# Down projections of a two-layer decoder step: 512 tokens in one matmul, the 8 sample tokens by a second, narrow path

## The chip, the cores and the metric

The kernel runs on one core of one Trainium2 chip. The metric is the device time of one execution in microseconds (us), here the median of several runs. Five engines matter: TensorE (PE in the profile, with its weight loads as a row of their own, PEld), VectorE (DVE), ScalarE (ACT), GpSimd (POOL) and SyncE (SP), which issues nearly all of the DMAs.

## The reference, cut to what matters

A group of 512 prompt tokens and a group of 8 sample tokens go through two layers with shared weights. Each layer has two feed-forward blocks, one ahead of the token mixer and one behind it:

```
D_MODEL, D_FF, SEQ = 1024, 2816, 512          # 8 sample tokens beside the 512
def swiglu(h, wg, wu, wd):
    return (jax.nn.silu(h @ wg) * (h @ wu)) @ wd

xp = xp + 0.5 * swiglu(rmsnorm(xp, norm_ffn1[i]), ffn1_wg[i], ffn1_wu[i], ffn1_wd[i])
xs = xs + 0.5 * swiglu(rmsnorm(xs, norm_ffn1[i]), ffn1_wg[i], ffn1_wu[i], ffn1_wd[i])
# then the mixer (attention in layer 0, a convolution module in layer 1),
# then the same once more with ffn2, then a gated per-layer input embedding
```

The product with `wd` (2816 x 1024) is the down projection. There are four of them: `down1` and `down2` of both layers. All inputs are fp32.

## The kernel before

**Layout.** The 520 tokens lie along the free dimension, features along the 128 partitions. `x` is `[128, 8, 520]`, the hidden values of a feed-forward block are `[128, 22, 520]` (22 groups of 128 features, `KF`).

**Arithmetic.** A product of fp32 values is made of three products of a format, fp32r, that TensorE takes in one pass: each operand is split into a high and a low part, and hi x hi, hi x lo and lo x hi are summed in PSUM (`products`, L253). The weights are split in the kernel: ScalarE copies a slab of raw weights into `w_hi` (`split_hi`, L238), and VectorE subtracts to get `w_lo` (`split_lo`, L242). A plain fp32 matmul, which the kernel uses in smaller places, is issued by the compiler as two instructions, so that for instance the 2 matmuls of `stat_pe` (L289) are 4 rows of the trace; a transpose stays one.

**Token halves.** A PSUM bank holds 512 fp32 columns, and 520 tokens don't fit. So each output tile takes two banks, 260 tokens in each, and each of the three products of a k group is issued twice, once for each half, with the same weights: 6 matmuls of 260 columns for each group of 128 features, each with its own weight load.

**A down projection** makes 8 output tiles (m) of 128 features. The weights of a tile come in two slabs of 11 k groups (`KH`; 128 x 1408 values). A slab is thus 66 matmuls, a projection 16 slabs and 1056 matmuls, and the four projections 64 slabs and 4224 matmuls. Two buffers `w_raw`, `w_hi` and `w_lo` (j = 0, 1) take the slabs in turn, and two PSUM slots (s = 0, 1; two banks each) take the tiles in turn.

**Who waits for whom in a down projection.** There is no planner; the order is written out for each engine, with counting semaphores between them.

- SP (`to_x_sp`, `load_slab`, L232): the load of slab n waits for `slab_lo`, until slab n - 2, which has the same buffer, is split. All weight loads of the kernel go through this one queue in order.
- ACT (`to_x_act`): `split_hi` of slab n waits for its landing and for `slab_used`, until PE is through with slab n - 2. Once a tile there are also `h_hi` (L264) and a square (L266) of the finished x tile.
- DVE (`to_x_dve`): in each tile two `split_lo`, `add_to_x` (L310), which adds half of the PSUM tile to x, and `h_lo` (L270) for the next stage.
- PE (`down_pe`): waits for `evac` of the tile that last had the slot, then for `slab_lo` and `a_lo_ok` of each slab, and issues `products`.

The last tile of a projection is evacuated during the first slab of the stage behind it (`after_to_x`), and the hidden values of the last group of an up stage (`after_up`) during the first slab of the down projection.

**Plain fp32 with quarters of the columns.** The kernel has places where a weight operand of 32 columns is used and the output goes to 32 of the 128 PSUM partitions, with the quarter g changing from one matmul to the next: `sample_values` (L962) in the attention and `taps_pe` (L1573) in the convolution. Both move 512 columns.

Of the kernel before, what the change touches and what calls it, by code (L numbers as in the profile page):

```python
# [5 lines left out]
F32 = mybir.dt.float32  # L6
# [42 lines left out]
def build(nc, io):  # L49
# [4 lines left out]
    with ctx:  # L54
# [35 lines left out]
        minus_bias = sb("minus_bias", [P, NH])  # L90
        eps = sb("eps", [P, 2])
        pages = sb("pages", [1, NS * PG], I32)


        def phase_memory(*specs):
# [6 lines left out]
            ("taps_j", [P, 4, KD, GROUPS], F32))  # L102
        a_hi, a_lo = phase_memory(("a_hi", [P, KF, T], F32R), ("a_lo", [P, KF, T], F32R))
        (o_hi, o_lo, k_f, sg_p, sg_m, a_t, kc, vc, zs, runs, aw) = phase_memory(
# [35 lines left out]
        def slot(s):  # L140
            return ps[:, s, :, 0:HALF]

        def flat(s, b=0):
# [40 lines left out]
        tap4_in = sem("tap4_in")  # L184
        ident4_ok = sem("ident4_ok")


        at = {}
        slab = tile = norm = hid = xt = fn = 0
        for layer in range(2):  # L190
            for name in (("load",) if layer == 0 else ()) + ("up1", "down1", "mix", "mixout", "up2", "down2", "ple"):
                at[name, layer] = dict(slab=slab, tile=tile, norm=norm, hid=hid, xt=xt, fn=fn)
                if name == "load":
# [8 lines left out]
                if name[:4] == "down":  # L202
                    slab += 2 * KD
                    tile += KD
                    xt += KD
                if name == "mix":
                    n = 3 * NP if layer == 0 else 2 * KD
                    slab += n
                    tile += n
                    fn += 0 if layer == 0 else KD  # L210
                    norm += 1
# [15 lines left out]

        def load_slab(sp, n, j, src, kt):

            sp.wait_ge(slab_lo, n - 1)  # L230
            dst = w_raw[:, j, 0:kt * P].rearrange("p (k c) -> p k c", k=kt)
            sp.dma_start(dst, src).then_inc(slab_in[j], 16)  # L232
# [12 lines left out]
        def products(pe, out, j, w0, kts, hi, lo, k0, first, last, wait_k=None, token_halves=(0, 1)):  # L245
# [168 lines left out]
        def to_x_sp(sp, a, spt, w, loaded=0):  # L414
            n0 = a["slab"]
            with sp.Fori(loaded // 2, KD * spt // 2) as step:
                m = 2 // spt * step
                for j in range(2):
                    src = slab_src(w, m, j * KH, KH) if spt == 2 else slab_src(w, m + j)
                    load_slab(sp, n0 + spt * m + j, j, src, KH if spt == 2 else KD)  # L420

# [26 lines left out]
        def to_x_dve(dve, a, spt, layer, which, factor, prev_evac, prev_lo):  # L448
# [5 lines left out]
            if spt == 2:  # L454
                def step(m, s):

                    split_lo(dve, n0 + 2 * m, 0, cols)
                    add_to_x(dve, s, n0 + 2 * m - 1, m - 1, factor)
                    split_lo(dve, n0 + 2 * m + 1, 1, cols)
                    x_post_dve(dve, a, layer, which, m - 1)  # L460
# [21 lines left out]
        def down_pe(pe, a, hidden):  # L482
            n0, t0 = a["slab"], a["tile"]
            with pe.Fori(0, KD // 2) as half:
                m = 2 * half
                for s in range(2):
                    pe.wait_ge(evac, t0 + m + s - 1)
                    for c in range(2):
                        pe.wait_ge(slab_lo, n0 + 2 * (m + s) + c + 1)
                        pe.wait_ge(a_lo_ok, hidden + KH * (c + 1))  # L490
                        products(pe, slot(s), c, 0, range(KH), a_hi, a_lo, c * KH, c == 0, c == 1).then_inc(slab_used, 1)

# [85 lines left out]

        def load_dve(dve):
            def x_in(m):  # L580
                dve.wait_ge(load_t, m + 1)
# [31 lines left out]
        def after_to_x(a, spt, layer, which, factor):  # L613
# [8 lines left out]
            def dve_evac(dve):  # L622
                def run_(j):
                    m = KD - 2 + j
                    if spt == 1 or j == 1:
                        add_to_x(dve, m % 2, a["slab"] + spt * (m + 1) - 1, m, factor)
                return run_
# [112 lines left out]
        def attn_sp(sp):  # L740
# [20 lines left out]
            for m in range(NP):  # L761
                load_slab(sp, n0 + m, m % 2, qkv_src(0, m), KD)
            sp.wait_ge(first_in[3], 16)
# [742 lines left out]
        def conv_sp(sp):  # L1506
            n0 = C["slab"]

            def both(k):
                for c in range(2):  # L1510
                    src = io["conv_w_in"][0].rearrange("(k p) f -> p k f", p=P)[:, :, ds(c * D + k * P, P)]
                    load_slab(sp, n0 + 2 * k + c, c, src, KD)

# [419 lines left out]
        def ple_sp(sp, a, layer):  # L1933
            n0 = a["slab"]
            for g in range(2):
                src = io["ple_w_proj"][layer].rearrange("(k p) f -> p k f", p=P)[:, :, g * 4 * P:(g + 1) * 4 * P]
                sp.wait_ge(slab_lo, n0 + g - 1)
                sp.dma_start(w_raw[:, g, 0:KP * 4 * P].rearrange("p (k c) -> p k c", k=KP), src).then_inc(slab_in[g], 16)
            with sp.Fori(0, KD // 2) as half:
# [290 lines left out]
```

## Time and profile before

| | |
|---|---|
| median of 3 runs | 2304.34 us (2300.72 to 2305.11) |
| the profiled execution, its own time | 2306.85 us |
| its span in the trace | 2305.1 us |
| PE busy | 2207.5 us, 96% of the span |
| DVE / ACT / POOL busy | 1099.3 / 752.8 / 152.4 us |
| mean granted TensorE clock | 0.981 of full speed |
| read from and written to HBM | 229.25 and 9.86 MB |

The trace is of one execution. Starts are recorded; ends of matmuls are modelled and neighbours overlap, so the pace of PE is read from the distance between starts, not from durations. In the timeline view neighbouring instructions of one line and one pair of operands are merged: the first column is the start of the first one, the second the time to the end of the last one, and "x2" their count. The clock column of the window view is the granted TensorE clock: 1.00 is 2.4 GHz, 0.50 is 1.2 GHz.

### The profile page before, as it was taken

The numbers are of one execution on the slowest core, as the hardware profiler recorded it, in microseconds if no ns is written. First come the engines' busy times: TensorE is split into PE (matmuls) and PEld (weight loads), VectorE is DVE, ScalarE is ACT, GpSimd is POOL, SyncE is SP. The second block draws the span as 40 slices with busy tenths as digits, with TensorE's granted clock in tenths as the row PEclk, the third lists the DMA queues.
The fourth block names the chain that finished last, engine by engine and source line by source line (L and its number), as shares of the span: only waits on it lengthen the run. The fifth ranks groups of instructions, "written<-read, shape, count | busy, mean of one in ns | idle before, by whom it ended". The sixth has DMA issues, their size and how long they took to land.

```text
span 2305.1 us, 43436 instructions
## 1 busy us (share of the span) xinstructions
PE 2207.5 (96%) x17957; PEld 2105.6 (91%) x17957; DVE 1099.3 (48%) x1280; ACT 752.8 (33%) x1012; POOL 152.4 (7%) x117
## 2 busy tenths in 40 slices
PE   7999999978998999999999999999798899999998
PEld 7999999967777999999999999999565899999998
DVE  5444433378884444443355444433635644443344
ACT  4222222446663422222234222222111532222223
POOL 2000001010000100000110000001302100000100
PEclk9999999989998999999999999999899899999999
DMA  3333332425663333333232333333454233333322
GB/s 115 91 91 91 105 88 81 156 92 186 218 229 112 100 91 91 91 105 88 81 92 83 91 91 91 100 92 90 125 124 118 58 92 91 91 91 101 93 71 83
DMA packets 379914, 240.30 MB, mean 104 GB/s; under 512 B 8506, under 2 KB 362394, under 8 KB 379832
## 3 DMA queue, kind: packets, MB, share of 16 engines
q1 hardware_dynamic: 371128, 234.89, 34.5%
q10 hardware_dynamic: 8704, 4.26, 0.6%
q8 instruction: 59, 0.97, 0.2%
q14 instruction: 23, 0.19, 0.0%
HBM read 229.25 MB, written 9.86 MB: 104 GB/s over the span
## 4 chain that ended last, share of the span: by engine, by line
PE 83%; DVE 7%; issue 4%; DMA 3%; ACT 2%; POOL 1%; ACTq 0%; SPq 0%; DVEq 0%; POOLq 0%
PE ps L253 79%; DVE sg_m L1341 1%; DMA g_rows<-g_pad 1%; DVE kc L1357 1%; PE ps L1573 1%; DVE w_lo L242 1%; PE ps L1969 1%; DVE sg_p L1348 1%; DVE zs L1362 1%; DMA g<-g_rows 1%; POOL log_ms L1918 0%; PE ps L825 0%; DMA w_raw<-in_attn_w_qkv 0%; ACT w_hi L238 0%; DVE h_lo L270 0%
## 5 line engine op out<-in xcount | busy, mean ns | idle before, releaser
L253 PE MATMUL ps<-h_hi,w_hi 128*128 128x260 f32 x3712 | 757.6, 285 | 15.0 <-DVE w_lo L242 10.4
L253 PE MATMUL ps<-h_hi,w_lo 128*128 128x260 f32 x3712 | 749.9, 284 | 0.0
L253 PE MATMUL ps<-h_lo,w_hi 128*128 128x260 f32 x3712 | 748.6, 283 | 0.0
L238 ACT ACTIVATE w_hi<-w_raw 128x1024 fp32r<-128x1024 f32 (+1 forms) x314 | 353.9, 1127 | 1122.5 <-PE ps L253 1092.2
L253 PEld LDWEIGHTS ps<-h_hi,w_hi 128*128 128x128 f32 x3712 | 575.3, 189 | 27.7 <-DVE w_lo L242 12.2
L253 PEld LDWEIGHTS ps<-h_hi,w_lo 128*128 128x128 f32 x3712 | 574.0, 189 | 0.0
L253 PEld LDWEIGHTS ps<-h_lo,w_hi 128*128 128x128 f32 x3712 | 573.0, 189 | 0.0
L242 DVE TENSOR_TENSOR w_lo<-w_raw,w_hi 128x1024 fp32r<-128x1024 f32 (+1 forms) x316 | 420.3, 1330 | 270.9 <-ACT w_hi L238 270.4
L253 PE MATMUL ps<-a_hi,w_hi 128*128 128x260 f32 x1408 | 283.9, 283 | 0.0
L253 PE MATMUL ps<-a_hi,w_lo 128*128 128x260 f32 x1408 | 283.2, 282 | 0.0
L253 PE MATMUL ps<-a_lo,w_hi 128*128 128x260 f32 x1408 | 282.7, 282 | 0.0
L304 DVE TENSOR_TENSOR s_up<-ps,rms 128x520 f32<-128x520 f32 x108 | 75.5, 699 | 321.5 <-PE ps L253 315.3
L253 PEld LDWEIGHTS ps<-a_lo,w_hi 128*128 128x128 f32 x1408 | 217.2, 188 | 0.0
L253 PEld LDWEIGHTS ps<-a_hi,w_hi 128*128 128x128 f32 x1408 | 216.8, 188 | 0.0
L253 PEld LDWEIGHTS ps<-a_hi,w_lo 128*128 128x128 f32 x1408 | 216.6, 188 | 0.0
L304 DVE TENSOR_TENSOR s_gate<-ps,rms 128x520 f32<-128x520 f32 x116 | 81.1, 699 | 187.4 <-PE ps L253 148.0
L310 DVE SCALAR_TENSOR_TENSOR x<-ps,x 128x520 f32 (+1 forms) x42 | 29.4, 700 | 199.9 <-PE ps L253 199.9
L283 POOL TENSOR_TENSOR sumsq<-sumsq,square 128x520 f32<-128x520 f32 x56 | 87.4, 1560 | 480.4 <-ACT square L266 450.1
L328 ACT ACTIVATE a_hi<-s_prod 128x520 f32 (+1 forms) x88 | 56.2, 639 | 176.2 <-DVE s_prod L335 176.2
L337 DVE TENSOR_TENSOR a_lo<-s_prod,a_hi 128x520 f32 (+1 forms) x88 | 61.6, 700 | 80.7 <-ACT a_hi L328 80.7
L280 POOL COPY sumsq<-square 128x520 f32<-128x520 f32 x8 | 6.8, 852 | 1384.7 <-ACT square L266 1360.0
L270 DVE SCALAR_TENSOR_TENSOR h_lo<-x,gains,h_hi 128x520 fp32r<-128x520 f32 (+1 forms) x64 | 80.5, 1266 | 3.4 <-ACT h_hi L264 2.0
(224 smaller groups left out, 1588.5 us busy)
## 6 DMA issues: line engine op xcount, KB each, us to landing
w_raw<-in_ffn_wg SPq DMA_DIRECT2D x88, 512.0 KB, 3.8
w_raw<-in_ffn_wu SPq DMA_DIRECT2D x88, 512.0 KB, 3.8
w_raw<-in_ffn_wd SPq DMA_DIRECT2D x64, 704.0 KB, 4.4
kc<-in_cache_k SPq DMA_DIRECT2D x32, 512.0 KB, 5.5
vc<-in_cache_v SPq DMA_DIRECT2D x28, 512.0 KB, 6.0
w_raw<-in_attn_w_qkv SPq DMA_DIRECT2D x24, 512.0 KB, 4.6
g<-g_rows SPq DMA_DIRECT2D x32, 268.0 KB, 4.7
w_raw<-in_ple_w_gate SPq DMA_DIRECT2D x16, 512.0 KB, 3.7
```

Source lines behind the costliest of these rows:

```text
L238: act.activation(w_hi[:, j, 0:cols], w_raw[:, j, 0:cols], ACT.Copy).then_inc(slab_hi, 1)
L242: dve.tensor_tensor(w_lo[:, j, 0:cols], w_raw[:, j, 0:cols], w_hi[:, j, 0:cols].bitcast(F32), ALU.subtract).then_inc(slab_lo, 1)
L253: ins = pe.matmul(out[:, b_, :], a[:, j, w], b[:, k0 + k, b_ * HALF:(b_ + 1) * HALF], start=(first and k == kts[0] and n == 0), stop=(last ...
L270: dve.scalar_tensor_tensor(h_lo[:, ds(m, 1), :].rearrange("p a t -> p (a t)"), x[:, ds(m, 1), :].rearrange("p a t -> p (a t)"), gain_col(l ...
L283: pool.tensor_tensor(sumsq[:, :], sumsq[:, :], square[:, m2, :], ALU.add).then_inc(acc_ok, 1)
L304: dve.tensor_tensor(halves(out), slot(s), halves(rms[:, :]), ALU.mult).then_inc(evac, 1)
L310: dve.scalar_tensor_tensor(xm, slot(s), factor, xm, ALU.mult, ALU.add).then_inc(evac, 1)
L328: act.activation(a_hi[:, ds(f, 1), :].rearrange("p a t -> p (a t)"), s_prod[:, :], ACT.Copy).then_inc(a_hi_ok, 1)
L337: dve.tensor_tensor(a_lo[:, ds(f, 1), :].rearrange("p a t -> p (a t)"), s_prod[:, :], a_hi[:, ds(f, 1), :].rearrange("p a t -> p (a t)").b ...
L1341: ins = dve.tensor_tensor_scan(m, m, zero[:, :].broadcast_to([P, (i + 1) * P]), 1.0, ALU.mult, ALU.max)
L1348: dve.tensor_tensor(sg_p[:, u, 0:TP - 1], sg_p[:, u, 0:TP - 1], sg_m[:, n % 4, 1:TP], ALU.mult).then_inc(a_ok, 1)
L1357: dve.tensor_tensor(kc[:, g, :], kc[:, g, :], q_bc, ALU.mult).then_inc(kq_ok, 1)
```

## The change

In the four down projections (nowhere else):

- **Tokens.** Each of the three products is issued once, with the 512 prompt tokens as one matmul of 512 columns into one bank (`products_wide`): 33 matmuls a slab instead of 66.
- **Samples.** The 8 sample tokens are the last of the 520. For each k group one plain fp32 matmul (`sample_rows`) takes the last 32 tokens' hidden values (`a_end`, 32 weight columns) against the raw weight slab (128 moving columns) and writes 32 tokens x 128 features to the PSUM quarter `g = k mod 4`, bank 1, columns 128 to 255 of the slot. 11 such matmuls stand ahead of the 33 wide ones in each slab, and their last one increments `small_mm`.
- **Turning.** The four quarters hold partial sums with tokens on partitions. `sample_part` (DVE) copies the 128 x 128 block to `log_ms`; then one fp32 matmul on PE with those 128 x 128 values as weights and `sample_sel` (128 x 8; it picks the last 8 of each 32 and adds the quarters) as moving operand gives 128 features x 8 samples, in the 8 columns behind the 512. PE waits for `small_ok` ahead of it, behind the second slab's wide matmuls; it increments `wide_mm`.
- **Evacuation.** `add_wide_to_x` waits for `wide_mm` instead of `slab_used` and reads the same 520 columns in one piece.
- **Hidden values.** `hidden_hi_act` gets one more ScalarE copy a group (128 x 32, 88 in all), `a_end`.
- **Loads.** Since PE now reads `w_raw`, a load of slab n in a down projection waits also for `small_mm`, until the sample matmuls of slab n - 2 are done; so do the first two loads of the stage behind each down projection (attention, convolution, up of the next block where it takes them over, and the embedding's `ple_sp`). The SP loop over the slabs is written out.
- **Once.** A VectorE reduction at the start makes `sample_sel` from the identity matrix.

```
+        def products_wide(pe, s, j, kts, hi, lo, k0, first, last):
+            for k in kts:
+                w = slice(k * P, (k + 1) * P)
+                for n, (a, b) in enumerate(((w_hi, hi), (w_hi, lo), (w_lo, hi))):
+                    ins = pe.matmul(ps[:, s, 0, :], a[:, j, w], b[:, k0 + k, 0:TP],
+                                    start=(first and k == kts[0] and n == 0), stop=(last and k == kts[-1] and n == 2))
+            return ins
+
+        def sample_rows(pe, s, j, kts, k0):
+            for k in kts:
+                g = (k0 + k) % 4
+                ins = pe.matmul(ps[g * Q:(g + 1) * Q, s, 1, P:2 * P], a_end[:, k0 + k, :],
+                                w_raw[:, j, k * P:(k + 1) * P], start=k0 + k < 4, stop=k0 + k >= KF - 4)
+            return ins
+
+        def sample_part(dve, s, n):
+            dve.wait_ge(small_mm, 2 * n + 2)
+            dve.tensor_copy(log_ms[:, 0:P], ps[:, s, 1, P:2 * P]).then_inc(small_ok, 1)

+        def add_wide_to_x(dve, a, s, m, factor):
+            dve.wait_ge(wide_mm, a["wd"] + m + 1)
+            xm = x[:, ds(m, 1), :].rearrange("p a t -> p (a t)")
+            dve.scalar_tensor_tensor(xm, wide(s), factor, xm, ALU.mult, ALU.add).then_inc(evac, 1)

         def load_slab(sp, n, j, src, kt, rows_read=None):
             sp.wait_ge(slab_lo, n - 1)
+            if rows_read is not None:
+                sp.wait_ge(small_mm, rows_read)

         def hidden_hi_act(act, a, f):
             act.wait_ge(prod_ok, a["hid"] + f + 1)
+            act.activation(a_end[:, ds(f, 1), :].rearrange("p a t -> p (a t)"), s_prod[:, T - Q:T], ACT.Copy)

         # to_x_dve, a step
                     split_lo(dve, n0 + 2 * m, 0, cols)
-                    add_to_x(dve, s, n0 + 2 * m - 1, m - 1, factor)
+                    sample_part(dve, s, a["wd"] + m - 1)
+                    add_wide_to_x(dve, a, s, m - 1, factor)
                     split_lo(dve, n0 + 2 * m + 1, 1, cols)

         # down_pe, a tile
                     for c in range(2):
                         pe.wait_ge(slab_lo, n0 + 2 * (m + s) + c + 1)
                         pe.wait_ge(a_lo_ok, hidden + KH * (c + 1))
-                        products(pe, slot(s), c, 0, range(KH), a_hi, a_lo, c * KH, c == 0, c == 1).then_inc(slab_used, 1)
+                        sample_rows(pe, s, c, range(KH), c * KH).then_inc(small_mm, 1)
+                        products_wide(pe, s, c, range(KH), a_hi, a_lo, c * KH, c == 0, c == 1).then_inc(slab_used, 1)
+                    pe.wait_ge(small_ok, a["wd"] + m + s + 1)
+                    pe.matmul(ps[:, s, 1, 0:NS], log_ms[:, 0:P], sample_sel[:, :], start=True, stop=True).then_inc(wide_mm, 1)

         # load_dve, first
+            dve.wait_ge(const_ok, 1)
+            dve.tensor_reduce(sample_sel[:, :], ident[:, :].rearrange("p (g c) -> p c g", g=4)[:, Q - NS:Q, :],
+                              AX.X, ALU.add).then_inc(sel_ok, 1)
```

## Rows read from the trace of the kernel before

**Rows 1.** The page: busy time by engine; lines of the chain that ended last.

```profile
PE 2207.5 (96%) x17957; PEld 2105.6 (91%) x17957; DVE 1099.3 (48%) x1280; ACT 752.8 (33%) x1012; POOL 152.4 (7%) x117
...
PE ps L253 79%; DVE sg_m L1341 1%; DMA g_rows<-g_pad 1%; DVE kc L1357 1%; PE ps L1573 1%; DVE w_lo L242 1%; PE ps L1969 1%; DVE sg_p L1348 1%; DVE zs L1362 1%; DMA g<-g_rows 1%; POOL log_ms L1918 0%; PE ps L825 0%; DMA w_raw<-in_attn_w_qkv 0%; ACT w_hi L238 0%; DVE h_lo L270 0%
```

**Rows 2.** The four down projections as windows: busy us and instructions by engine.

```profile
core 0: us, PE busy (x) PEld busy (x) DVE busy (x) ACT busy (x) POOL busy (x), PEclk, DMA share, GB/s
280.90:407.80 126.90, 126.90 (x1060) 126.90 (x1059) 43.93 (x33) 30.46 (x31) 10.32 (x7) 1.00 0.31 90
...
2102.30:2229.20 126.90, 126.90 (x1060) 126.90 (x1059) 42.70 (x32) 30.46 (x31) 10.33 (x7) 1.00 0.29 86
sum 507.60, PE 507.60 PEld 507.60 DVE 173.26 ACT 121.82 POOL 41.32; mean PE 126.90 PEld 126.90 DVE 43.32 ACT 30.46 POOL 10.33
```

**Rows 3.** Timeline of PE in a down projection: start, us, line, operands, count.

```profile
299.90 0.40 PE L253 MATMUL ps<-a_lo,w_hi 128*128 128x260 f32 x2
...
300.62 0.40 PE L253 MATMUL ps<-a_lo,w_hi 128*128 128x260 f32 x2
```

**Rows 4.** Timeline of PE in a stretch at half the clock, and its window.

```profile
1799.83 0.64 PE L253 MATMUL ps<-c_lo,w_hi 128*128 128x260 f32 x2
...
1802.43 0.64 PE L253 MATMUL ps<-c_lo,w_hi 128*128 128x260 f32 x2
...
1799.80:1804.20 4.40, 4.40 (x23) 4.40 (x22) 3.98 (x7) 4.31 (x7) 0.00 (x0) 0.50 0.02 4
```

**Rows 5.** Timeline of PE around four plain fp32 passes of 260 columns (L289).

```profile
413.16 0.40 PE L253 MATMUL ps<-h_hi,w_lo 128*128 128x260 f32 x2
413.39 1.04 PE L289 MATMUL ps<-sumsq,ones 128*128 128x260 f32 x4
414.08 0.59 PE L253 MATMUL ps<-h_hi,w_hi 128*128 128x260 f32 x2
414.51 0.40 PE L253 MATMUL ps<-h_lo,w_hi 128*128 128x260 f32 x2
```

**Rows 6.** Timeline of PE around fp32 matmuls in column quarters, in the attention.

```profile
554.05 0.40 PE L253 MATMUL ps<-h_hi,w_lo 128*128 128x260 f32 x2
554.38 1.92 PE L962 MATMUL ps<-vc,aw 128*32 128x512 f32 x16
556.24 0.51 PE L253 MATMUL ps<-h_hi,w_hi 128*128 128x260 f32 x2
556.58 0.41 PE L253 MATMUL ps<-h_lo,w_hi 128*128 128x260 f32 x2
```

**Rows 7.** The same around the quarters of the convolution's last taps.

```profile
1745.70 0.40 PE L253 MATMUL ps<-h_hi,w_lo 128*128 128x260 f32 x2
1746.03 6.22 PE L1573 MATMUL ps<-g,diag 128*32 128x512 f32 x56
1752.17 0.51 PE L253 MATMUL ps<-h_hi,w_hi 128*128 128x260 f32 x2
1752.52 0.41 PE L253 MATMUL ps<-h_lo,w_hi 128*128 128x260 f32 x2
```

**Rows 8.** Matmuls of 128 and of 1 moving columns (timeline of PE; L925 are transposes).

```profile
529.54 1.91 PE L925 MATMUL ps<-ident,sg_p 128*128 128x128 f32 x16
...
567.00 0.95 PE L973 MATMUL ps<-ones,w_raw 128*128 128x1 f32 x8
567.81 0.92 PE L973 MATMUL ps<-ones,square 128*128 128x1 f32 x7
```

**Rows 9.** Timeline of DVE, then ACT, then SP, in one tile of a down projection.

```profile
312.96 0.70 DVE L310 SCALAR_TENSOR_TENSOR x<-ps,x 128x520 f32 x1 [5.02 <-PE ps L253]
314.25 1.63 DVE L242 TENSOR_TENSOR w_lo<-w_raw,w_hi 128x1408 fp32r<-128x1408 f32 x1 [0.59 <-ACT w_hi L238]
...
312.83 1.38 ACT L238 ACTIVATE w_hi<-w_raw 128x1408 fp32r<-128x1408 f32 x1 [6.55 <-PE ps L253]
...
316.03 0.37 SPq L232 DMA_DIRECT2D w_raw<-in_ffn_wd  x1
```

**Rows 10.** The source line of the slab loads, 290 to 380 us: issue to landing.

```profile
DMA to landing us min/median/max: 4.2/4.4/4.5
```

**Rows 11.** Timeline of DVE behind the first down projection.

```profile
407.87 0.70 DVE L310 SCALAR_TENSOR_TENSOR x<-ps,x 128x520 f32<-128x520 f32 x1 [5.55 <-PE ps L253]
409.02 1.23 DVE L242 TENSOR_TENSOR w_lo<-w_raw,w_hi 128x1024 fp32r<-128x1024 f32 x1 [0.46 <-ACT w_hi L238]
410.17 0.75 DVE L270 SCALAR_TENSOR_TENSOR h_lo<-x,gains,h_hi 128x520 fp32r<-128x520 f32 x1
```

**Rows 12.** Short instructions of ACT and DVE, by line and form: count, busy us, mean ns.

```profile
L1211 ACT ACTIVATE w_raw<-zs 128x64 f32<-128x64 f32 x8 | 2.0, 247 | 0.7 <-DVE zs L1368 0.7
...
L588 DVE COPY taps<-ps 128x248 f32<-128x248 f32 x1 | 0.4, 405 | 0.0
L1762 DVE TENSOR_REDUCE ident<-ident 128x32 f32<-128x128 f32 x1 | 0.3, 321 | 0.0
```

More of the change, by code:

```diff
@@ L91, in build @@
         eps = sb("eps", [P, 2])
+        sample_sel = sb("sample_sel", [P, NS])
         pages = sb("pages", [1, NS * PG], I32)
@@ L102, in build @@
             ("taps_j", [P, 4, KD, GROUPS], F32))
-        a_hi, a_lo = phase_memory(("a_hi", [P, KF, T], F32R), ("a_lo", [P, KF, T], F32R))
+        a_hi, a_lo, a_end = phase_memory(("a_hi", [P, KF, T], F32R), ("a_lo", [P, KF, T], F32R), ("a_end", [P, KF, Q], F32))
         (o_hi, o_lo, k_f, sg_p, sg_m, a_t, kc, vc, zs, runs, aw) = phase_memory(
@@ L141, in slot, with wide @@
             return ps[:, s, :, 0:HALF]
+        def wide(s):
+            return ps[:, s, :, :].rearrange("p b n -> p (b n)")[:, 0:T]
         def flat(s, b=0):
@@ L185, in build @@
         ident4_ok = sem("ident4_ok")
+        sel_ok = sem("sel_ok")
+        small_mm = sem("small_mm")
+        small_ok = sem("small_ok")
+        wide_mm = sem("wide_mm")
         at = {}
-        slab = tile = norm = hid = xt = fn = 0
+        slab = tile = norm = hid = xt = fn = wd = 0
         for layer in range(2):
             for name in (("load",) if layer == 0 else ()) + ("up1", "down1", "mix", "mixout", "up2", "down2", "ple"):
-                at[name, layer] = dict(slab=slab, tile=tile, norm=norm, hid=hid, xt=xt, fn=fn)
+                at[name, layer] = dict(slab=slab, tile=tile, norm=norm, hid=hid, xt=xt, fn=fn, wd=wd)
                 if name == "load":
@@ L205, in build @@
                     xt += KD
+                    wd += KD
                 if name == "mix":
@@ L224, in gain_col, with load_slab @@
             return gains[:, ds((which * 2 + layer) * KD + m, 1)]
-        def load_slab(sp, n, j, src, kt):
+        def load_slab(sp, n, j, src, kt, rows_read=None):
             sp.wait_ge(slab_lo, n - 1)
+            if rows_read is not None:
+                sp.wait_ge(small_mm, rows_read)
             dst = w_raw[:, j, 0:kt * P].rearrange("p (k c) -> p k c", k=kt)
@@ L415, in to_x_sp @@
             n0 = a["slab"]
[L416 to L420, printed above, removed]
+            if spt == 2:
+                for n in range(2 * KD):
+                    load_slab(sp, n0 + n, n % 2, slab_src(w, n // 2, n % 2 * KH, KH), KH,
+                              2 * a["wd"] + n - 1 if n > 1 else None)
+            else:
+                with sp.Fori(loaded // 2, KD // 2) as step:
+                    m = 2 * step
+                    for j in range(2):
+                        load_slab(sp, n0 + m + j, j, slab_src(w, m + j), KD)
         def to_x_act(act, a, spt, layer, which, prev):
@@ L483, in down_pe @@
             n0, t0 = a["slab"], a["tile"]
+            pe.wait_ge(sel_ok, 1)
             with pe.Fori(0, KD // 2) as half:
@@ L624, in run_ @@
                     m = KD - 2 + j
-                    if spt == 1 or j == 1:
-                        add_to_x(dve, m % 2, a["slab"] + spt * (m + 1) - 1, m, factor)
+                    if spt == 1:
+                        add_to_x(dve, m % 2, a["slab"] + m, m, factor)
+                    elif j == 0:
+                        sample_part(dve, (KD - 1) % 2, a["wd"] + KD - 1)
+                    else:
+                        add_wide_to_x(dve, a, m % 2, m, factor)
                 return run_
@@ L761, in attn_sp @@
             for m in range(NP):
-                load_slab(sp, n0 + m, m % 2, qkv_src(0, m), KD)
+                load_slab(sp, n0 + m, m % 2, qkv_src(0, m), KD, 2 * M["wd"] - 1 + m if m < 2 else None)
             sp.wait_ge(first_in[3], 16)
@@ L1511, in both @@
                     src = io["conv_w_in"][0].rearrange("(k p) f -> p k f", p=P)[:, :, ds(c * D + k * P, P)]
-                    load_slab(sp, n0 + 2 * k + c, c, src, KD)
+                    load_slab(sp, n0 + 2 * k + c, c, src, KD, 2 * C["wd"] - 1 + c if isinstance(k, int) and k == 0 else None)
             def shifted(k):
@@ L1937, in ple_sp @@
                 sp.wait_ge(slab_lo, n0 + g - 1)
+                sp.wait_ge(small_mm, 2 * a["wd"] - 1 + g)
                 sp.dma_start(w_raw[:, g, 0:KP * 4 * P].rearrange("p (k c) -> p k c", k=KP), src).then_inc(slab_in[g], 16)
```

## The prediction

> **What bounds the kernel now.** I read the page first. PE is busy for 96% of the span, and of the chain that ended last 79% is one line, L253, the products [rows 1]. Next come the windows over the four down projections [rows 2]: PE and its weight loads are busy for every microsecond of the 126.90 us of each, at full clock, while DVE works 43 us and ACT 30 us. So inside the changed stages nothing but PE counts, and there its pace: 126.90 / 1056 = 120.2 ns for a matmul of 260 columns, 240.3 ns for the two halves. The timeline says the same: six starts in 300.62 - 299.90 = 0.72 us [rows 3]. The question is therefore plain: what does PE take for a wide matmul, and what for the sample path. The profiled execution took 2306.85 us, 2.5 us over the median of 2304.34; the sum below is a difference, and I put it on the median.
>
> **What a matmul of 512 columns takes.** At half the clock (1.2 GHz) six pairs of 260 columns take 1802.43 - 1799.83 = 2.60 us [rows 4], 216.7 ns each: one column a cycle and nothing on top. At 2.4 GHz the columns would be 108.3 ns, and 120.2 is measured. The 12 ns are no cost of columns if the weight load sets that pace: one-column matmuls with 128 x 128 weights follow each other in about 0.11 us (from 567.00 to 567.81 there are eight starts, the first two nearly together, so seven steps of 0.11) [rows 8]. Where the columns take longer than a load, the load vanishes: four plain fp32 passes of 260 columns lie between 413.16 + 0.24 = 413.40 and 414.51 - 0.24 = 414.27, 0.87 us or 218 ns each [rows 5], two cycles a column (216.7) and about 1 ns, each pass with its own weight load. 520 column slots in 218 ns make 512 slots 214.6; I take 215.0. The lower bound is 512 / 2.4 = 213.3 ns. The upper one takes the 260-column pace as a price by the column: 120.2 x 512 / 260 = 236.7 ns. I take the value near the lower end, because the fp32 passes show a stream of just this length with loads under it.
> Saved: 240.3 - 215.0 = 25.3 ns for each of 2112 pairs, 53.4 us (bounds 57.0 and 7.6).
>
> The Trainium skill has a rule that would make far more of it. In "TensorE: Matmul & The Clock Gate", section "Back-to-back issue gap", it gives a sustained pace in real kernels of about 131 ns for a matmul of 512 columns, against 216 ns for one on its own. No run so far shows a full-array matmul faster than a column a cycle; by the rule the saving would be 231 us instead of 53, and it has its place among the rivals.
>
> **What the samples' matmuls take.** A slab has 11 fp32 matmuls in quarters, 22 instructions. Two rows have such quarters between ordinary pairs. In the attention: the pair ahead would end its turn at 554.05 + 0.24 = 554.29, the first undisturbed pair behind it starts at 556.58, so the first pair should have begun at 556.34; the block costs 2.05 us for 16 instructions [rows 6]. In the convolution: 1745.94 to 1752.28, 6.34 us for 56 [rows 7]. The difference is 4.29 us for 40 instructions, 107 ns each; 512 columns at two cycles are 427 ns, so four instructions run at once and make a round of 0.429 us. 4 rounds and 14 rounds leave 2.05 - 1.72 = 0.33 us and 6.34 - 6.01 = 0.33 us: a fixed price of going into the quarters and out of them. PE's loads lie idle in it.
> With 128 columns a round should be a quarter: 0.107 us by columns; transposes of 128 fp32 columns take (1.91 - 0.30) / 15 = 0.107 us [rows 8]. I take 0.109, a nanosecond or two for the step. 11 matmuls over four quarters give three matmuls to the fullest, six passes: 6 x 0.109 = 0.65 us, and the fixed 0.33 us once a slab: 0.98 us. The slab's wide matmuls are full-array ones, so both crossings are paid for every slab. 64 x 0.98 = 62.9 us. Bounds: nothing for the crossings, 0.65 x 64 = 41.9 us; hi and lo passes that don't pair up across quarters, 12 rounds, 1.64 x 64 = 105 us.
>
> **The turning matmul.** Two passes of 8 columns with 128 x 128 weights, 32 times. The first load lies under the wide matmul ahead of it, the second is open: 0.11 us and 0.02 us of passes, 0.13 x 32 = 4.2 us. Upper bound: both loads and half a crossing more, 0.4 us or 13 us. Fp32 passes over the full array beside fp32r ones cost no crossing [rows 5].
>
> **What lies beside other work.**
> - PE's wait for `small_ok`. The copy to `log_ms` stands on DVE behind a `split_lo`, which in the tile shown begins 1.4 us after PE has released ACT for the split (312.83) and ends 3.1 us after it [rows 9]; every slab has this beat; the copy itself is under 0.4 us (248 columns take 405 ns) [rows 12]. It is done some 3.7 us into a slab of 8.1; the wait is met. Were that cover gone, PE and behind it the next tile would stand by the lateness, and `add_wide_to_x` with it.
> - The loads. A load is issued as soon as the split that frees its buffer is done, at 316.03 [rows 9], and lands in at most 4.5 us [rows 10]; it is needed a slab and more later. With `small_mm` it is issued 0.98 us into the PE time of slab n - 2, lands at 5.5, and `split_hi` can't begin before that slab ends at 8.1: 2.6 us to spare, and 4 us more until PE needs it. Behind the waiting load SP's queue holds only the next slab loads. At the border the second load of the next stage is issued some 7 us before the projection ends and lands 2.6 us before it.
> - ACT's 88 copies of 32 columns (under 0.25 us, 64 columns take 247 ns) and DVE's 32 copies: 22 and 13 us on engines that idle for most of these stages [rows 2, 12]. The reduction at the start (0.32 us) runs while the inputs are on their way.
> - The end of a projection. Evacuation waits for the turning matmul, 0.2 us later than for the last product. In the next stage the last `h_lo` ends at 410.92, and PE needs it for k = 7 of the first tile, 7 x 0.72 = 5.0 us after its start at 407.67, at 412.7 [rows 11]: 1.8 us to spare.
>
> **Sum.** 62.9 + 4.2 - 53.4 = +13.7 us: 2304.3 + 13.7 = 2318 us. What is won on the wide matmuls is spent on the samples: 8 of 520 tokens cost PE an eighth of each slab's time.
>
> **The rivals.**
> - **Crossings hidden** (faster). PE takes the quarter's loads ahead while the last wide matmuls stream, and the full load during the last round. The sum is then 41.9 + 4.2 - 53.4 = -7.3 us, 2297 us. It decides from a fixed price of 0.33 - 13.7 / 64 = 0.12 us a slab. Against it: the same 0.33 in both rows, one of them [rows 7] with nothing else for PE to wait for. 8 in 100, and 6 in 100 for something between that ends within 0.2% (4.6 us) of the present time, about what a measurement of this kernel can tell from no change.
> - **Columns cost what they cost now.** 236.7 ns, saved 7.6, +59.5 us, 2364 us. For it: nothing in the trace is an fp32r matmul of another width. Against it: the half-clock pace and the fp32 passes. 6 in 100.
> - **Twelve rounds instead of six.** Short passes might not be ready in fours: +42 us, 2360 us. Against: loads of 32 columns overlap freely in the rows. 4 in 100.
> - **A late slab.** From a landing time of 4.4 + 2.6 = 7.0 us on, ACT starts late, and from about 11 us on PE stands; each us over it costs up to 64 us. 4.2 to 4.5 us is the whole spread. 1 in 100.
> - **Wide matmuls overlap one another in the array.** If the next one streamed before the last is through, the weight load would set the pace of the wide ones as it does of the narrow ones, 120.2 ns: saved 2112 x (240.3 - 120.2) = 254 us, 2304.3 + 67.1 - 254 = 2118 us. Against it: half-clock rows and fp32 passes both stand exactly at the column rate [rows 4, 5]. 1 in 100. The page of the Trainium skill named above supports this one; by its figure it would be 2140 us.
> - My forecast holds the other 74.
>
> **Chances and range.** The likeliest case alone spans 2310 to 2332 us: wide matmuls of 213.3 to 218 ns (-4 to +6 us), crossings of 0.28 to 0.40 us (-3 to +4), turning up to 0.4 us (+9). The range goes down to 2303 for the partly hidden crossings and up to 2336. Faster 0.08, within 0.2% 0.07, slower 0.85: all cases but the hidden crossings and the overlap are slower.
>
> **What the changed profile would show.** Wide matmuls of 128x512 in the down projections at 215 ns from start to start, right if 213 to 217, wrong at 236 or 131. Blocks of 22 instructions 128*32 128x128 in six groups of starts 0.109 us apart. 0.33 us of overhead around each block; the loads' row has its gaps there. Two passes of 8 columns in about 0.13 us once a tile. No idle time of PE behind a DVE copy or a landing. A projection of 126.9 + 3.4 = 130.3 us. The forecast is wrong if PE waits in the projections, if the clock falls in them, or if another stage changes its length.

## The result and the profile after

The changed kernel takes 2358.35 us (median of 4 runs, 2354.34 to 2358.62), the kernel before beside it 2304.46 us: the ratio is 1.0232, 95% interval 1.022 to 1.0244. It is slower, as forecast, but by 54 us and not by 14; the time lies outside the range of 2303 to 2336.

The page of the changed kernel, the rows that answer to [rows 1]. L274 are the wide matmuls, L283 the sample blocks, L264 the unchanged products:

```profile
PE 2254.5 (96%) x17317; PEld 2037.0 (86%) x17317; DVE 1106.7 (47%) x1313; ACT 764.8 (32%) x1100; POOL 152.5 (6%) x117
...
PE ps L264 56%; PE ps L274 21%; PE ps L283 2%; DVE sg_m L1397 1%; DMA g_rows<-g_pad 1%; PE ps L1629 1%; DVE w_lo L253 1%; PE ps L2026 1%; ACT sg_p L1240 1%; DVE sg_p L1404 1%; DMA g<-g_rows 1%; ACT sg_m L1236 1%; DVE kc L1413 0%; POOL log_ms L1974 0%; PE ps L881 0%
```

The four projections as windows, answering to [rows 2]:

```profile
281.40:420.70 139.30, 139.30 (x897) 110.18 (x897) 45.59 (x41) 30.55 (x32) 10.29 (x7) 1.00 0.30 84
...
sum 557.00, PE 557.00 PEld 440.64 DVE 179.93 ACT 122.17 POOL 41.15; mean PE 139.25 PEld 110.16 DVE 44.98 ACT 30.54 POOL 10.29
```

A projection takes 139.3 us instead of 126.9, at full clock, and PE is busy in all of it. The weight loads are not any more (110 of 139 us): fewer loads under longer matmuls. Counted from the first start of each projection to the first start of the stage behind it, the four take 557.1 us instead of 506.9, 50.2 us more. Between the two profiled executions the difference is 2358.33 - 2306.85 = 51.5 us; the rest of the spans, outside the projections, differs by about 1 us, and the remaining 2.5 us are the distance of the profiled execution of before to its median. So nearly the whole change sits in the projections, without waits. The timeline of PE from the first block to the second tile says where:

```profile
281.11 0.40 PE L264 MATMUL ps<-h_hi,w_lo 128*128 128x260 f32 x2
281.43 0.85 PE L283 MATMUL ps<-w_raw,a_end 128*32 128x128 f32 x22
282.22 0.50 PE L274 MATMUL ps<-a_hi,w_hi 128*128 128x512 f32 x1
282.56 0.39 PE L274 MATMUL ps<-a_lo,w_hi 128*128 128x512 f32 x1
...
298.40 0.40 PE L274 MATMUL ps<-a_hi,w_lo 128*128 128x512 f32 x1
298.64 0.28 PE L539 MATMUL ps<-sample_sel,log_ms 128*128 128x8 f32 x2
298.85 0.85 PE L283 MATMUL ps<-w_raw,a_end 128*32 128x128 f32 x22
...
299.98 0.39 PE L274 MATMUL ps<-a_lo,w_hi 128*128 128x512 f32 x1
...
300.90 0.40 PE L274 MATMUL ps<-a_hi,w_lo 128*128 128x512 f32 x1
...
307.18 0.40 PE L274 MATMUL ps<-a_hi,w_lo 128*128 128x512 f32 x1
307.51 0.85 PE L283 MATMUL ps<-w_raw,a_end 128*32 128x128 f32 x22
308.29 0.50 PE L274 MATMUL ps<-a_hi,w_hi 128*128 128x512 f32 x1
308.63 0.39 PE L274 MATMUL ps<-a_lo,w_hi 128*128 128x512 f32 x1
```

A tile repeats after 298.85 - 281.43 = 17.42 us, where it was 126.9 / 8 = 15.86. The block of 22 lasts 0.79 us from its first start to the first wide start, and the crossings lie around it, as in [rows 6, 7]. The turning matmul adds little: from the last wide matmul ahead of a block to the second one behind it there are 308.63 - 307.18 = 1.45 us in the middle of a tile and, with the turning matmul between, 299.98 - 298.40 = 1.58 us, so it costs the 0.13 us that the prediction gave it. But the wide matmuls follow each other in (300.90 - 299.98) / 4 = 0.230 us, not in 0.215. Over longer stretches it is 232 ns (e1 below: 11 steps in 2.55 us). 2112 of them at 17 ns are the 36 us that the prediction missed.

### The profile page after: what moved, and what is told of

Read it like the earlier page. It is cut to its first block, busy times and chain, and to the rows that moved or that the text cites. A ratio compares the mean times of both kernels' runs of the same rounds, so it can differ in the third digit from the quotient of the medians.

```text
span 2356.5 us, 42211 instructions
## 1 busy us (share of the span) xinstructions
PE 2254.5 (96%) x17317; PEld 2037.0 (86%) x17317; DVE 1106.7 (47%) x1313; ACT 764.8 (32%) x1100; POOL 152.5 (6%) x117
## 4 chain that ended last, share of the span: by engine, by line
PE 84%; DVE 6%; issue 4%; ACT 2%; DMA 2%; POOL 1%; ACTq 0%; SPq 0%; DVEq 0%; POOLq 0%
PE ps L264 56%; PE ps L274 21%; PE ps L283 2%; DVE sg_m L1397 1%; DMA g_rows<-g_pad 1%; PE ps L1629 1%; DVE w_lo L253 1%; PE ps L2026 1%; ACT sg_p L1240 1%; DVE sg_p L1404 1%; DMA g<-g_rows 1%; ACT sg_m L1236 1%; DVE kc L1413 0%; POOL log_ms L1974 0%; PE ps L881 0%
## 5 line engine op out<-in xcount | busy, mean ns | idle before, releaser
L264 PE MATMUL ps<-h_hi,w_hi 128*128 128x260 f32 x3712 | 757.6, 285 | 14.3 <-DVE w_lo L253 9.7
L264 PE MATMUL ps<-h_hi,w_lo 128*128 128x260 f32 x3712 | 750.1, 284 | 0.0
L264 PE MATMUL ps<-h_lo,w_hi 128*128 128x260 f32 x3712 | 748.8, 283 | 0.0
L264 PEld LDWEIGHTS ps<-h_hi,w_hi 128*128 128x128 f32 x3712 | 575.5, 189 | 27.0 <-DVE w_lo L253 11.6
L264 PEld LDWEIGHTS ps<-h_hi,w_lo 128*128 128x128 f32 x3712 | 574.5, 189 | 0.0
L264 PEld LDWEIGHTS ps<-h_lo,w_hi 128*128 128x128 f32 x3712 | 573.3, 189 | 0.0
L274 PE MATMUL ps<-a_hi,w_hi 128*128 128x512 f32 x704 | 284.4, 404 | 0.0
L274 PE MATMUL ps<-a_hi,w_lo 128*128 128x512 f32 x704 | 277.8, 395 | 0.0
L274 PE MATMUL ps<-a_lo,w_hi 128*128 128x512 f32 x704 | 277.2, 394 | 0.0
L274 PEld LDWEIGHTS ps<-a_hi,w_hi 128*128 128x128 f32 x704 | 132.0, 187 | 41.0 <-issue 12.7
L274 PEld LDWEIGHTS ps<-a_hi,w_lo 128*128 128x128 f32 x704 | 132.1, 188 | 31.3
L274 PEld LDWEIGHTS ps<-a_lo,w_hi 128*128 128x128 f32 x704 | 132.2, 188 | 28.6
L349 DVE SCALAR_TENSOR_TENSOR x<-ps,x 128x520 f32 (+1 forms) x32 | 22.4, 700 | 185.7 <-PE ps L539 185.7
L1629 PE MATMUL ps<-g,diag 128*32 128x512 f32 x448 | 59.0, 685 | 23.7 <-DMA g<-g_rows 19.6
```

The costliest lines, as they stand in the source:

```text
L264: ins = pe.matmul(out[:, b_, :], a[:, j, w], b[:, k0 + k, b_ * HALF:(b_ + 1) * HALF], start=(first and k == kts[0] and n == 0), stop=(last ...
L274: ins = pe.matmul(ps[:, s, 0, :], a[:, j, w], b[:, k0 + k, 0:TP], start=(first and k == kts[0] and n == 0), stop=(last and k == kts[-1] an ...
L1629: ins = pe.matmul(ps[g * Q:(g + 1) * Q, 3, k % 2, :], diag4[:, k, g, i, :], g4[:, k % 2, g, 4 * i:4 * i + TP], start=i == 0, stop=i == GRO ...
```

## The experiments

Seven runs (e1 to e4, e8, e10, e11) tell apart whether the 17 ns belong to the wide matmul alone or are done to it by the sample path, and what they are; four more (e7, e6, e5, e9) are about the sample path and ways to make it cheaper. The changed kernel, e1, e5, e7 and e9 were run four times each, the others once: what those say is read from their traces, where the granted clock in the first projection, from which the lines below are, is 1.00.

**e1, the wide matmuls alone.** Starting from the kernel before:

```
-  products(pe, slot(s), c, 0, range(KH), a_hi, a_lo, c * KH, c == 0, c == 1).then_inc(slab_used, 1)
+  products_wide(pe, s, c, range(KH), a_hi, a_lo, c * KH, c == 0, c == 1).then_inc(slab_used, 1)
-  add_to_x(dve, s, n0 + 2 * m - 1, m - 1, factor)          # 520 tokens, two banks
+  add_prompt_to_x(dve, s, n0 + 2 * m - 1, m - 1, factor)   # 512 tokens, bank 0
```

> The kernel before with one part of the change alone: the 512 prompt tokens as one matmul of 512 columns. The down projections leave out the 8 sample tokens altogether (their x stays as it was). My theory (the wide matmul takes 232.3 ns, not 215, and the sample path adds the rest): each projection is 528 x 232.3 = 122.7 us instead of 126.7, in all -16 us, 2288 us. The rival from the prediction's sum (215 ns, the missing 40 us come from the sample path disturbing the wide matmuls, for instance through reads of the raw slab or the switched array): 528 x 215 = 113.5 us, -53 us, 2251 us.

Measured: 2287.95 us, ratio 0.9925 (0.9908 to 0.9942), 16 us faster. The first window of e1, the first projection:

```profile
281.00:403.60 122.60, 122.60 (x530) 99.10 (x529) 43.90 (x33) 30.45 (x31) 10.33 (x7) 1.00 0.32 93
```

And its timeline of PE, eleven steps apart:

```profile
299.82 0.39 PE L318 MATMUL ps<-a_hi,w_hi 128*128 128x512 f32 x1
...
302.37 0.39 PE L318 MATMUL ps<-a_hi,w_lo 128*128 128x512 f32 x1
```

122.60 / 528 = 232.2 ns, and eleven steps in 2.55 us say the same. The 17 ns are the wide matmul's own, whether the sample path is there or not.

**e2, other widths.** The probe kernels e2 to e4, e10 and e11 are e1 with the form of the matmuls chosen by slab position, one PSUM group a slab:

```
+  for a, b, k, w in terms(j, j, a_hi, a_lo):
+      t = 0
+      for i, width in enumerate(widths):      # (512,), (256, 256), (384, 128), (448,)
+          jobs.append((i % 2, ps[:, s, i % 2, 0:width], a[:, j, w], b[:, j * KH + k, t:t + width]))
+          t += width
```

> As e1, but the four slab positions (tile parity, slab) move 512 columns in one matmul; 256 + 256 into two banks; 384 + 128 into two banks; and 448 in one. Only one group a slab is summed, so the down projections' result is not the reference's. Theory columns (an fp32r column costs 0.446 ns at full clock, 1.07 cycles, and 4 ns a matmul come on top): 512 at 232, 256 at 118 to 120, 384 + 128 together about 175 + 112 = 287, 448 at 204 ns. Theory loads (the weight load under a matmul takes about 19 ns of its stream, whatever its width): 256 at 126, 384 + 128 at 179 + 112, 448 at 206. Theory of a rate that holds only up to some length (a buffer that runs dry late in a long stream): 448 well under 204, 384 near 162.

Measured: 2302.28 us. From its timeline:

```profile
288.61 0.40 PE L333 MATMUL ps<-a_hi,w_hi 128*128 128x256 f32 x2
...
296.15 0.40 PE L333 MATMUL ps<-a_hi,w_lo 128*128 128x256 f32 x2
...
298.62 0.45 PE L333 MATMUL ps<-a_hi,w_lo 128*128 128x384 f32 x2
...
300.62 0.44 PE L333 MATMUL ps<-a_hi,w_hi 128*128 128x384 f32 x2
...
307.65 0.36 PE L333 MATMUL ps<-a_hi,w_hi 128*128 128x448 f32 x1
...
309.88 0.36 PE L333 MATMUL ps<-a_hi,w_lo 128*128 128x448 f32 x1
```

256 + 256: 32 steps of a pair in 7.54 us, 117.8 ns a matmul. 384 + 128: 7 steps in 2.00 us, 286 ns the two. 448: 11 steps in 2.23 us, 203 ns. With 512 at 232 and 260 at 120 everything that was run with 256 columns or more lies close to one line, 0.446 ns a column and 4 ns a matmul; 384 columns by that line (175 ns) and a weight load of 0.11 us [rows 8] make up the 286, so the 128 columns of the split pair don't hide the next load. A fixed 17 or 19 ns would have given 126 for 256. So it is a price by the column, 1.07 cycles.

**e3, places.** Two PSUM banks in turn; weights from one place; moving values from one place; both.

```
+  bank = i % 2 if what == "banks" else 0
+  wt = w_hi[:, j, 0:P] if what in ("weights", "both") else a[:, j, w]
+  mv = a_hi[:, j * KH, 0:TP] if what in ("moving", "both") else b[:, j * KH + k, 0:TP]
```

> As e1, 512 columns everywhere, but by slab position: consecutive matmuls alternate between two PSUM banks; the weights come always from one place; the moving operand comes always from one place; both from one place. Results of the down projections are not the reference's. Theory bank (adding to the same bank of PSUM as the matmul before costs the 17 ns): 215 with two banks, 232 in the others. Theory places (reads of weights and moving values collide by address): two banks 232, one of the fixed positions clearly away from 232, above all both fixed, and no scatter from matmul to matmul there. Theory columns: 232 in all four.

Measured: 2286.98 us; the window over the whole projection, and its timeline of PE:

```profile
280.10:402.20 122.10, 122.10 (x529) 99.03 (x528) 43.81 (x33) 30.45 (x31) 10.26 (x7) 1.00 0.33 93
...
280.02 0.39 PE L333 MATMUL ps<-a_hi,w_hi 128*128 128x512 f32 x1
...
296.04 0.62 PE L333 MATMUL ps<-a_hi,w_hi 128*128 128x512 f32 x2
...
302.85 8.11 PE L333 MATMUL ps<-a_hi,w_hi 128*128 128x512 f32 x34
310.80 0.39 PE L333 MATMUL ps<-a_lo,w_hi 128*128 128x512 f32 x1
```

The mean over the four positions is 231.3 ns, against 232.2 in e1, but it hides that they differ. Two banks and weights from one place (with the first three of the next position 69 steps, 296.04 - 280.02 = 16.02 us) take 232 ns: neither the bank nor the place of the weights is it. With the moving values from one place, 30 steps take 302.85 - 296.04 = 6.81 us, 227 ns; after the first few every step is 226 or 227 ns, where in the first two positions and in e1 they vary from 225 to 239 ns. With both from one place, which for the moving values is another one, 34 steps take 7.95 us, 234 ns. So with the place of the moving values up to 5 of the 17 ns go and up to 2 come; the rest doesn't hang on any place that was tried.

**e4, forms.** fp32r; bf16; fp32r with 64 weight columns; plain fp32.

```
+  if what == "bf16":  wt, mv = probe_b[:, 0:P], probe_b[:, :]
+  if what == "64":    wt, out = a[:, j, k * P:k * P + 64], ps[0:64, s, 1, :]
+  if what == "fp32":  wt, mv = wt.bitcast(F32), mv.bitcast(F32)
```

> As e1, but by slab position: fp32r as in the change; bf16 weights and moving values of 512 columns; fp32r with 64 instead of 128 weight columns (half a weight load); plain fp32, two passes of 512 columns. Results of the down projections are not the reference's. Theory columns (the cost is that of reading fp32r values at one column a cycle): fp32r 232, bf16 215 to 216, 64 weight columns 232, fp32 428 a pass. Theory loads: bf16 lower than 232 as its load is shorter, 64 weight columns about 223, fp32 a pass 427 + 17. Theory power or clock (the array holds back under load): bf16 near 232 too.

Measured: 2607.97 us (the fp32 position takes four times the cycles). Timeline:

```profile
289.87 7.29 PE L333 MATMUL ps<-probe_b 128*128 128x512 bf16 x33
...
297.23 0.40 PE L333 MATMUL ps<-a_lo,w_hi 128*64 128x512 f32 x1
...
304.45 0.39 PE L333 MATMUL ps<-a_hi,w_lo 128*64 128x512 f32 x1
...
305.54 1.02 PE L333 MATMUL ps<-a_lo,w_hi 128*128 128x512 f32 x2
...
308.11 1.02 PE L333 MATMUL ps<-a_lo,w_hi 128*128 128x512 f32 x2
```

bf16: (7.29 - 0.38) / 32 = 216 ns. Half a weight load: 31 steps in 7.22 us, 233 ns, no gain. fp32: 6 passes in 2.57 us, 428 ns each, two cycles a column and 1 or 2 ns. Of these forms only fp32r, with a new four-byte value in every cycle, pays clearly more than its columns.

**e8, zeros.**

```
-  act.activation(a_hi[:, ds(f, 1), :]..., s_prod[:, :], ACT.Copy)
+  act.activation(a_hi[:, ds(f, 1), :]..., s_prod[:, :], ACT.Copy, scale=0.0)     # and a_lo = a_hi - a_hi
```

> As e1, but all hidden values, high and low, are zero in the down projections (the results are not the reference's). Theory power (the array holds back with the number of bits that switch): wide matmuls at 215 ns instead of 232, the whole 36 us under e1, near 2252 us. Theory columns (the reading of fp32r values is the limit, whatever they are): 232 ns, 2288 us.

Measured: 2289.4 us, and in its windows again 122.60 us a projection. With moving values that are all zero the price is the same, so it isn't the number of bits that switch.

```profile
281.40:404.00 122.60, 122.60 (x530) 99.10 (x529) 43.90 (x33) 30.46 (x31) 10.32 (x7) 1.00 0.32 93
```

**e10, a step in memory.** fp32r; bf16 with every second value; fp32r; bf16 in one piece.

```
+  flat_b = probe_b[:, :, :].rearrange("p t e -> p (t e)")            # probe_b [P, TP, 2] bf16
+  wt, mv = flat_b[:, 0:P], flat_b[:, 0:TP] if what == "bf16" else probe_b[:, :, 0]
```

> As e4, with the slab positions: fp32r; bf16 with every second of 1024 values moved (the same bytes are stepped over as with fp32r); fp32r; bf16 in one piece. Results of the down projections are not the reference's. Theory columns, in its form that the port reads memory at a rate a little under four bytes a cycle: bf16 at a step of four bytes 232 ns, in one piece 216. In its other form (the fp32r format itself takes 1.07 cycles a column in the array): both bf16 positions 216, fp32r 232.

Measured: 2273.77 us. Four strided bf16 matmuls, and the block in one piece with 32 of its 33 records:

```profile
288.17 1.06 PE L333 MATMUL ps<-probe_b 128*128 128x512 bf16 x4
...
303.30 7.07 PE L333 MATMUL ps<-probe_b 128*128 128x512 bf16 x32
```

With the step (1.06 - 0.38) / 3 = 227 ns (226 over the slab), in one piece (7.07 - 0.38) / 31 = 216. Ten of the 17 ns come with the step alone, at the same format. That was between the two forms of the theory, so one more run:

**e11, steps.** fp32r at a step of 8 bytes; fp32r with no step, one value for all columns; fp32r; bf16 at 8 bytes.

```
+  if what == "one":    mv = b[:, j * KH + k, 0:1].broadcast_to([P, TP])
+  if what == "apart":  mv = (every second of the 1024 values from group k on)
```

> As e10 (bf16: 216 ns in one piece, 226 with a step of four bytes; fp32r 232), with the slab positions: fp32r with every second of 1024 values moved (a step of 8 bytes); fp32r with one and the same value for all 512 columns (no step at all); fp32r as in the change; bf16 with a step of 8 bytes. Results of the down projections are not the reference's. Theory memory (the pace is set by the bytes of memory that the moving operand is stepped over): fp32r well over 232, perhaps twice the excess of 17 ns, at 8 bytes; 215 to 216 without a step; bf16 at 8 bytes over 226. Theory format (fp32r itself takes 1.07 cycles a column, and the 10 ns of the bf16 step are a thing of their own): fp32r 232 in all three.

Measured: 2517.35 us. Timeline: first 8 bytes, then one value, then bf16 at 8 bytes:

```profile
289.86 0.63 PE L333 MATMUL ps<-a_hi,w_lo 128*128 128x512 f32 x1
...
297.10 0.40 PE L333 MATMUL ps<-a_hi,w_hi 128*128 128x512 f32 x1
...
297.55 0.38 PE L333 MATMUL ps<-a_hi,w_lo 128*128 128x512 f32 x1
...
300.36 0.38 PE L333 MATMUL ps<-a_hi,w_hi 128*128 128x512 f32 x1
...
311.90 15.07 PE L333 MATMUL ps<-probe_b 128*128 128x512 bf16 x33
```

| moving operand, 512 columns | bytes a column | ns a matmul | run |
|---|---|---|---|
| fp32r, one value | 0 | 216 (2.81 us / 13) | e11 |
| bf16 | 2 | 216 | e4, e10 |
| bf16, every second | 4 | 226 | e10 |
| fp32r | 4 | 232 | e1 |
| fp32r, every second | 8 | 453 (7.24 us / 16) | e11 |
| bf16, every fourth | 8 | 451 ((15.07 - 0.63) / 32) | e11 |

The runs fit a pace that is set by the stretch of SBUF that the moving operand runs over, whatever its format: up to 2 bytes a column it is a column a cycle, and at the steps of 8 and of 4 bytes bf16 comes out at one and the same rate, 4096 / 451 = 9.1 and 2048 / 226 = 9.1 bytes a nanosecond and partition. fp32r asks for 4 bytes each 0.417 ns, 9.6 a nanosecond, just more than that. No other steps were run, and what in the read path sets this rate no run shows. Why fp32r stands at 232 in the change and not at the 226 of bf16 with the same step stays open too; e3 has a hint, since with all moving values from one place, as in the bf16 runs, it took 227 in one place and 234 in another.

**e7, the sample path alone.** The changed kernel with the halves of 260 columns put back:

```
-  products_wide(pe, s, c, range(KH), a_hi, a_lo, c * KH, c == 0, c == 1).then_inc(slab_used, 1)
+  products(pe, slot(s), c, 0, range(KH), a_hi, a_lo, c * KH, c == 0, c == 1).then_inc(slab_used, 1)
   # the quarters and the turned values go to ps[:, 2, s, ...]; x is added from slot(s)
```

> The other part alone: the halves of 260 columns stay as in the kernel before, and the whole sample path is added beside them (its PSUM block in two banks that the projections don't use; its results are computed and turned, but x takes the samples from the halves). My theory (the two parts add up): 64 x 0.985 + 32 x 0.11 = +66.6 us against the kernel before, 2371 us. Rival (the sample path also slows the products beside it, and the wide matmuls of the change suffer from that): more than 2371, by up to 36 us, and starts of the 260-column matmuls further apart than 120 ns.

Measured: 2371.85 us, ratio 1.0295 (1.0278 to 1.0313); 143.40 us a projection, PE busy in all of it. (143.40 - 126.90) / 16 = 1.03 us a slab, where the prediction's terms make 0.98 + 0.07 = 1.05.

**e6, two blocks a slab.**

```
-  sample_rows(pe, s, c, range(KH), c * KH).then_inc(small_mm, 1)
+  sample_rows(pe, s, c, range(4), c * KH)
+  (wide matmuls of k 0 to 3)
+  sample_rows(pe, s, c, range(4, KH), c * KH).then_inc(small_mm, 1)
```

> The changed kernel with each slab's 11 sample matmuls in two blocks, 4 ahead of the first four k groups and 7 ahead of the other seven. 4 matmuls are 2 rounds and 7 are 4 rounds, so the rounds stay six. Theory crossing: one more crossing a slab, 64 x 0.33 = +21.4 us, 2379.8 us. Rival (crossings are free, and the first round of a block is slow): the same time as the changed kernel.

Measured: 2381.11 us, 22.8 us over the changed kernel; 144.4 us a projection, so (144.4 - 139.3) / 16 = 0.32 us for one more crossing with the rounds unchanged.

**e5, one block a tile.**

```
-  sample_rows(pe, s, c, range(KH), c * KH).then_inc(small_mm, 1)
+  if c == 1:
+      for c_ in range(2):
+          sample_rows(pe, s, c_, range(KH), c_ * KH).then_inc(small_mm, 1)
```

> The changed kernel with the sample matmuls of both slabs of a tile in one block, ahead of the second slab's wide matmuls: 22 fp32 matmuls in a row, one crossing into the quarters and back for each tile instead of two. Theory crossing (each block pays 0.33 us beside its rounds): 32 x 0.33 = -10.7 us against the changed kernel, 2347.7 us. Rival (the 0.33 us grows with the block, or PE then waits for the next slab, whose load is issued a slab's sample time later): no gain, 2358 us or more; the trace would show PE idle before the first wide matmul of a tile behind w_lo.

Measured: 2358.75 us, no gain: the rival's time. A wait that the kernel before and the changed one don't show stands in the table of waits (idle us, count, longest):

```profile
ACT w_hi L249 <- DMA w_raw<-in_ffn_wd: 305.1, 28, 11.7
```

In its timeline ACT and DVE run late, here in the projection's fourth tile:

```profile
347.71 1.38 ACT L249 ACTIVATE w_hi<-w_raw 128x1408 fp32r<-128x1408 f32 x1 [11.36 <-DMA w_raw<-in_ffn_wd]
...
349.13 1.63 DVE L253 TENSOR_TENSOR w_lo<-w_raw,w_hi 128x1408 fp32r<-128x1408 f32 x1 [10.68 <-ACT w_hi L249]
350.67 0.28 DVE L289 COPY log_ms<-ps 128x128 f32<-128x128 f32 x1
```

The block began at 341.75; the raw slab is free only behind its first half, the load lands near 347.7, the split ends at 350.76, the copy at 350.95. The timeline of PE at that place:

```profile
350.72 0.40 PE L274 MATMUL ps<-a_hi,w_lo 128*128 128x512 f32 x1
351.01 0.39 PE L541 MATMUL ps<-sample_sel,log_ms 128*128 128x8 f32 x2
351.68 0.47 PE L274 MATMUL ps<-a_hi,w_hi 128*128 128x512 f32 x1 [0.28 <-issue]
351.99 0.39 PE L274 MATMUL ps<-a_lo,w_hi 128*128 128x512 f32 x1
```

The turning matmul starts 0.06 us behind the end of the copy and 0.29 us behind the last wide one, and the next tile's first wide matmul 0.67 us after it; in e9 below the two distances are 0.24 and 0.14 us. (The 0.31 us to the second wide matmul are no part of the loss: in e9 they are 0.32.) The tiles lose between nothing and 0.6 us; from the first turning matmul of this projection to the eighth e5 takes 122.46 us and e9 120.31, so 0.31 us a tile, about as much as one crossing had given. What comes too late is the copy: in four of the seven tiles it ends 0.06 us ahead of the turning matmul, and where it ends 0.33 us ahead or more nothing is lost. The rival had put the idle time behind `w_lo`; the trace puts it down to "issue", and e9 shows that the split is not what PE waits for.

**e9, the copy ahead of the split.** Against e5:

```
-  split_lo(dve, n0 + 2 * m, 0, cols)
   sample_part(dve, s, a["wd"] + m - 1)
+  split_lo(dve, n0 + 2 * m, 0, cols)
```

> As e5, one block a tile, and the copy of the sample block to log_ms stands on VectorE ahead of the split of the next slab instead of behind it. In e5 the load of a tile's next first slab is issued only when the block has read the raw slab, lands late, and split and copy both end when PE needs them: the turning matmul started up to 0.14 us late and the next tile's first matmul 0.2 us late. Theory (both waits together ate the 10.7 us): without the wait of the copy some 0.1 us a tile come back, the rest stays with the split: 2350 to 2357 us. Rival (only the copy mattered): the full gain, 2347 to 2348 us. Other rival (only the split mattered): no change from 2358.8.

Measured: 2350.51 us, ratio 1.0204 (1.0187 to 1.0221) against the kernel before, 8 us under the changed kernel. Its timeline of PE at the end of a tile:

```profile
297.37 0.40 PE L274 MATMUL ps<-a_hi,w_lo 128*128 128x512 f32 x1
297.61 0.28 PE L541 MATMUL ps<-sample_sel,log_ms 128*128 128x8 f32 x2
297.75 0.48 PE L274 MATMUL ps<-a_hi,w_hi 128*128 128x512 f32 x1
298.07 0.40 PE L274 MATMUL ps<-a_lo,w_hi 128*128 128x512 f32 x1
```

A projection takes 137.4 us from its first start to that of the next stage, 1.9 less than in the changed kernel, of 2.6 that a crossing in every tile is worth. The time lies at the lower end of what the theory of two waits gave, but that is luck: all tiles of the first projection end as the one above, 17.19 us apart, and PE waits in none, although the splits end only 0.5 to 0.7 us ahead of the next wide matmul. So the copy alone had been the wait. The rest of the gain goes to the turning matmul: it now stands between two wide ones and costs 298.07 - 297.37 = 0.70 us less two steps of 0.232, 0.23 us, where ahead of a block it cost 0.13. 0.33 - 0.10 = 0.23 us a tile are 1.9 us a projection. It is the best form of the change that was run, and still 47 us slower than the kernel before.

## Why the prediction was wrong

- **The step that failed** is the one under "What a matmul of 512 columns takes": "I take 215.0", "because the fp32 passes show a stream of just this length with loads under it". They do, but at one new value in two cycles, which asks the memory for half of what fp32r asks for. It took column slots for the measure where bytes a nanosecond were, and the half-clock rows [rows 4] have the same fault: there too the operand is read at half the rate. The one row that had the full rate was the 260-column pace itself, and I had explained its 12 ns away by the weight load, which at 112 ns happens to lie just below. Measured: 232 ns, saved 16.9 us instead of 53.4; and the same fp32r matmul with one value for all its columns takes the forecast's 216 ns (e11).
- With that term the prediction's own sum is 62.9 + 4.2 - 16.9 = +50.2 us, and the projections grew by 50 us.
- The rival **"Columns cost what they cost now"** was the right one: 236.7 ns, 2364 us. I gave it 6 in 100, and cut the range below it, though nothing in the trace was an fp32r matmul of another width. An upper bound that rests on the only row of the same format deserved more than one built from another format.
- **The sample path** held in its size and its parts. Six rounds of 22 instructions and 0.33 us of crossing: 1.03 us a slab with the turning matmul (e7), 0.32 us for a crossing by itself (e6), 0.13 us for a turning matmul in the changed kernel. The Trainium skill says it in "TensorEngine Tiling (Array Packing)", section "Key Properties": a change of the tiling mode drains the array. The runs agree as far as the price goes and put 0.32 us on it; that the array drains they don't show.
- **Cover.** No wait appeared in the changed kernel: the copy to `log_ms` was done long ahead, the loads too, although one took 5.7 us to land instead of at most 4.5 [rows 10]. e5 shows what a load issued a slab later does: it lands so late that the copy behind its split keeps PE waiting.
- **Crossings hidden, twelve rounds, a late slab**: none happened. Nor did wide matmuls overlap one another: the Trainium skill's 131 ns ("TensorE: Matmul & The Clock Gate", "Back-to-back issue gap") is met by no run here; bf16 stands at 216 ns, fp32r at 232.

## What to carry to other kernels

Ask of a matmul's pace which of three it is, and test the price on a row of the same format at the full clock: columns, the weight load, or the bytes that the moving operand reads in a nanosecond. When two of them give nearly the same number, as here 112, 108 and 116 ns for 260 columns, a change of width parts them, and the forecast has to keep both. A few leftover columns that ride along in a wide matmul are cheap (by the line above 8 columns in each of 33 products are 0.12 us a slab, an estimate); taken out, 8 of 520 tokens cost 1.03 us a slab of 7.9 here, four times what the wider matmuls gave back.

## What was not expected of the hardware

- fp32r at 2.4 GHz doesn't reach a column a cycle: 0.446 ns a column and 4 ns a matmul, for 256 to 512 columns, whatever the values, the PSUM bank, the weight columns or the place of the weights (e1 to e4, e8). The place of the moving values shifts the 232 ns for 512 columns to 227 or 234 (e3).
- Moving operands of bf16 slow down by their step too: 216, 226 and 451 ns for 2, 4 and 8 bytes. The Trainium skill ("SBUF — State Buffer", section "Door 1: The DMA port swizzle") says that a step stays free as long as two reads fall into one line of 16 bytes. For TensorE's moving operand the runs say otherwise: at 8 bytes, two to a line, the time doubles.
